# Four of six barriers a layer become waits for data; the beginning, the GDN preparation and the join to the SSM scan put in another order

## The chip, the cores and the metric

The kernel runs on one core of a Trainium2 chip. A core has five engines with an instruction queue each: TensorE (PE, matrix products), VectorE (DVE), ScalarE (ACT), GpSimd (POOL) and SyncE (SP, which here only starts DMA transfers and waits). They meet by semaphores. SBUF has 128 partitions; PE writes into PSUM, here eight banks of 512 f32 a partition. The metric is the time of the whole program on the device in microseconds, lower is better.

## The reference, cut to what matters

One inference step of two layers with three token mixers side by side. There are 1024 latent tokens and 128 context tokens, the model width is 1024.

```python
for l in range(DEPTH):                                   # DEPTH = 2
    shift, scale, gate = modulation(cond, w_mod[l], b_mod[l])   # silu(cond) @ w_mod + b_mod, cond: c and c_ctx
    h = rms_norm(x, norm_w[l]) * (1.0 + scale) + shift
    proj = einsum('btd,de->bte', h, w_in)                # one wide projection, split into all mixers' inputs
    # A: conv, silu, l2_normalize, gated delta rule, forward and backward, in chunks of 64
    o_a = rms_norm(o_f + rev(o_b), gdn_norm_w) * silu(a_z)
    # B: attention of 8 heads over 1152 keys (8 x 128 latent, 128 cached), 2 KV heads, rotary on q and k
    o_att = blocked_attention(q, keys, vals) * silu(b_z)
    # C: Mamba-2 scan, forward and backward, 16 heads of 64, state of 128
    y = rms_norm((y_f + rev(y_b) + ssm_d * c_x) * silu(c_z), ssm_norm_w)
    merged = sigmoid(g_a)*(o_a @ w_branch_a) + sigmoid(g_b)*(o_att @ w_branch_b) + sigmoid(g_c)*(y @ w_branch_c)
    x = x + gate * (merged @ w_out)
y = rms_norm(x, final_norm_w)                            # also returned: k, v and the states of the context
```

The latent tokens' scans begin from given states (`state_gdn`, `state_ssm`).

## The kernel before, in words

**Tiles and program.** The tokens are 9 tiles of 128 (NT = 9): 8 latent ones (NS = 8) and the context tile, number 8. Every engine has its own written program; both layers run in a loop (`Fori(0, DEPTH)`) of the same code. The order on an engine is the order of the code, and between engines only semaphores hold. Wide products are made of three f32r products (`h_hi`, `h_lo` by `w_hi`, `w_lo`, lines 819 to 821 and 1297 to 1299).

**Stages of a layer** (times of layer 1 from the timeline): beginning to 75 us; projection to 1025; GDN preparation 1031 to 1099; attention 1100 to 1360; SSM preparation 1362 to 1476; SSM scan 1477 to 1544; GDN scan 1545 to 1665; branches, gates and output product to about 2007. Between the first six stages stand barriers (line 590, quoted below): an engine drains, counts up `phase_done` and waits until all five have. There are six a layer (NPH = 6): 1 before the GDN preparation, 2 before attention, 3 before the SSM preparation, 4 before the SSM scan, 5 behind it, 6 behind the GDN scan.

```python
def barrier(e, l, k):                                    # line 590
    e.sem_inc(waits_held, 1)
    e.drain().then_inc(phase_done, 1)
    e.wait_ge(phase_done, l * 5 * NPH + 5 * k)
    e.sem_inc(waits_held, 1)
```

**Beginning.** SP loads nine token tiles, then four parts of layer 1's `w_mod` (2 MB each, line 851). PE turns the tokens (1129), makes a modulation product for each part (`mod_product`, 1142: eight k summed one after the other into partitions 0 and 1 of a bank), the norm's sums (1136) between the second and the third, turns 16 blocks of `mod_rows` (1161), and turns the vector constants `vec_in` (1187). ACT copies the products to `mod_rows` (1784). POOL loads the constants (`vec_load`, 22 transfers); `rows` and `qk_gain` are spread over 128 partitions by their DMAs. In layer 2 the modulation has been made during layer 1 with `mod_parts` (1149) and `mod_gather` (1155): 256 columns at a time from `w_next`, the k in four groups of partitions (`k % 4 * 32`), and the groups summed by a product with `pick`.

**GDN preparation.** For each tile PE makes the decay exponents (1318, 1319) from `g_row` and `g_col`, turns the 12 blocks of `gin` (1328) and makes k·k and k·q (1333, 1334); ACT exponentiates (1928) and squares (1936); POOL raises sums to a power; DVE makes the last product into `g_out` (2612); SP stores `g_out` (936), behind six loads into `beta_p` that wait for POOL's `g_clear`.

**Attention** ends with the context tile; **SSM preparation** makes for each tile the masks, `w_ssm`, `x_dt` and `x_rest` (DVE 2767, POOL 2300), the products `y_products` (1442), and beside it the next layer's modulation (`next_columns`). SP stores what the scans need (`tokens_out`). `xy_p_d` is where DVE's and ACT's solved blocks of the GDN are stored.

**SSM scan.** PE turns the first states `s_io` (1505) and makes a step for each tile in both directions: `c_t` by the state (1513), `xs` for its update (1518); POOL makes `s_kept` (2318), DVE the new state (2785). SP loads `xs` and `c_t` (`ssm_loads`, 1015 and 1017). ACT's queue loads the GDN scan's first tiles (`g_XY` by line 707, behind POOL's memsets and `g_clear`, since only blocks on its diagonal are filled), and ACT copies the last context state to `s_io` (2007).

## Time and profile before

| | |
|---|---|
| three runs | 3976.14, 3976.3, 3981.64 us, median 3976.3 |
| the profiled execution | 3979.19 us, its span 3977.4 us |
| granted PE clock | 0.971 of full speed, mean |
| busy PE, PEld | 3704.6 us (93%), 3471.8 us (87%) |
| busy DVE, ACT, POOL | 2056.2 us (52%), 1091.3 us (27%), 666.6 us (17%) |

PE is busy in 93% of the span, but not evenly: in 40 equal slices of it the page gives 6 tenths for the first, 7 for the two with the GDN preparations, 8 or 9 (90% and more) for the others. The chain that ended last tells for each piece of time which engine, queue or transfer the end waited for.

### The profile page before, as it was taken

To read this page: it belongs to the slowest core of one execution; us is meant where nothing else is said; L and a number is where in the kernel's file an instruction comes from. 1 tells how busy PE (TensorE), PEld (TensorE's weight loads), DVE (VectorE), ACT (ScalarE), POOL (GpSimd) and SP (SyncE) were. 2 spreads that over 40 slices of the span, in tenths; PEclk is the share of its full clock that TensorE was granted. 3 is DMA by queue.
4 is the path that set the end of the run, shared out by engine and by line. 5 is a ranking of instruction groups with operands and counts; after the bars stand their busy time and mean duration, and the time that the engine had idled before them with its cause. 6 is when DMAs were issued, how large, how long until landed. Compare 5 with 4: busy or idle time off the path is not lost.

```text
span 3977.4 us, 71786 instructions
## 1 busy us (share of the span) xinstructions
PE 3704.6 (93%) x29139; PEld 3471.8 (87%) x29139; DVE 2056.2 (52%) x2517; ACT 1091.3 (27%) x1952; POOL 666.6 (17%) x738
## 2 busy tenths in 40 slices
PE   6999999999789898899989999999997998988998
PEld 3999999999778775899989999999996886588998
DVE  3631354133478776575365215523326877746743
ACT  3211111122345461322122111111224456232320
POOL 1110111122310133101011101112233003510100
PEclk8999999999899999999989999999998999999999
...
GB/s 227 99 111 90 75 89 87 91 109 118 223 81 39 118 256 261 234 161 95 90 110 111 93 89 84 90 89 105 108 111 222 55 34 237 268 230 194 132 92 88
DMA packets 370673, 516.40 MB, mean 130 GB/s; under 512 B 83088, under 2 KB 293832, under 8 KB 367408
## 3 DMA queue, kind: packets, MB, share of 16 engines
...
q8 instruction: 222, 3.64, 0.4%
...
## 4 chain that ended last, share of the span: by engine, by line
PE 70%; issue 11%; DVE 7%; DMA 4%; DVEq 2%; ACT 2%; POOL 1%; SPq 1%; ACTq 0%; POOLq 0%
PE PSUM L819 10%; PE PSUM L820 10%; PE PSUM L821 10%; PE PSUM L1297 4%; PE PSUM L1299 4%; PE PSUM L1298 4%; PE PSUM L1382 3%; PE PSUM L1369 3%; PE PSUM L1539 2%; PE PSUM L1348 2%; PE PSUM L1671 1%; PE PSUM L1672 1%; PE PSUM L1673 1%; PE PSUM L1349 1%; DMA c_t<-proj_d 1%
## 5 line engine op out<-in xcount | busy, mean ns | idle before, releaser
L819 PE MATMUL PSUM<-h_hi,w_hi 128*128 128x384 f32 x2400 | 807.3, 336 | 8.2 <-DVEq L2513 8.2
L821 PE MATMUL PSUM<-h_hi,w_lo 128*128 128x384 f32 x2400 | 805.0, 335 | 0.0
L820 PE MATMUL PSUM<-h_lo,w_hi 128*128 128x384 f32 x2400 | 805.0, 335 | 0.0
L819 PEld LDWEIGHTS PSUM<-h_hi,w_hi 128*128 128x128 f32 x2400 | 453.3, 189 | 12.7 <-DVEq L2513 8.9
L820 PEld LDWEIGHTS PSUM<-h_lo,w_hi 128*128 128x128 f32 x2400 | 453.3, 189 | 0.0
L821 PEld LDWEIGHTS PSUM<-h_hi,w_lo 128*128 128x128 f32 x2400 | 453.1, 189 | 0.0
L2196 POOL DMA_DIRECT2D proj_d<-leave x140 | 132.3, 945 | 1438.1 <-DVE leave L2509 568.7
L1297 PE MATMUL PSUM<-h_hi,w_hi 128*128 128x384 f32 x960 | 325.1, 339 | 0.0
L1298 PE MATMUL PSUM<-h_lo,w_hi 128*128 128x384 f32 x960 | 321.2, 335 | 0.0
L1299 PE MATMUL PSUM<-h_hi,w_lo 128*128 128x384 f32 x960 | 321.2, 335 | 0.0
L2619 DVE TENSOR_REDUCE row_max<-PSUM 128x1 f32<-128x1152 f32 x128 | 173.4, 1355 | 101.3 <-PE PSUM L1349 101.1
L803 DVE CAST w_hi<-w_raw 128x2048 fp32r<-128x2048 f32 x56 | 68.6, 1224 | 256.3 <-PE PSUM L821 252.0
L1382 PE MATMUL PSUM<-v_all,prob_t 128*64 128x64 f32 x4608 | 165.5, 227 | 20.6 <-DVE o_bz L2696 15.8
L1382 PEld LDWEIGHTS PSUM<-v_all,prob_t 128*64 128x64 f32 x4608 | 148.0, 140 | 41.7 <-issue 21.1
L1297 PEld LDWEIGHTS PSUM<-h_hi,w_hi 128*128 128x128 f32 x960 | 180.4, 188 | 0.1
L1298 PEld LDWEIGHTS PSUM<-h_lo,w_hi 128*128 128x128 f32 x960 | 180.5, 188 | 0.0
L1299 PEld LDWEIGHTS PSUM<-h_hi,w_lo 128*128 128x128 f32 x960 | 180.2, 188 | 0.0
L2512 DVE SCALAR_TENSOR_TENSOR leave<-leave,PSUM 128x1152 f32<-128x1152 f32 x32 | 43.3, 1353 | 260.3 <-ACT leave L1842 260.0
L1348 PE MATMUL PSUM<-k_hi,q_tile 128*128 128x512 f32 (+1 forms) x384 | 145.8, 380 | 17.8 <-SPq L593 11.4
L1369 PE MATMUL PSUM<-cst,prob 128*128 128x128 f32 x1152 | 154.3, 280 | 8.3 <-DVE prob_t L2713 6.2
L1947 ACT ACTIVATE prob<-PSUM,row_max 128x1152 f32<-128x1152 f32 x128 | 155.8, 1217 | 14.9 <-DVE row_max L2619 14.5
L1950 ACT ACTIVATE prob_t<-PSUM 128x640 f32<-128x640 f32 x128 | 90.1, 704 | 247.0 <-PE PSUM L1369 247.0
...
## 6 DMA issues: line engine op xcount, KB each, us to landing
...
```

Source lines behind the costliest of these rows:

```text
L819: pe.matmul(dst, wh, x_hi[:, k, lo:hi], start=(k == 0), stop=False)
L820: pe.matmul(dst, wh, x_lo[:, k, lo:hi], start=False, stop=False)
L821: last = pe.matmul(dst, wl, x_hi[:, k, lo:hi], start=False, stop=(k == kt - 1))
L1297: pe.matmul(dst, wh, h_hi[:, k, at], start=(k == 0), stop=False)
L1298: pe.matmul(dst, wh, h_lo[:, k, at], start=False, stop=False)
L1299: last = pe.matmul(dst, wl, h_hi[:, k, at], start=False, stop=(k == KT - 1))
L1348: pe.matmul(dst, q_tile[t % 2][:, h], k_hi[:, g, col:col + width], start=True, stop=False)
L1369: last = pe.transpose(dst, prob[s][:, j * P:(j + 1) * P], ident)
L1382: last = pe.matmul(bank(7, AD, h * AD)[half], prob_t[s][:, j, half], v_all[:, kt, g * AD:(g + 1) * AD], start=(j == 0), stop=(j == len(sam ...
L1947: act.activation(prob[s][:], PSUM[:, 1536 * s:1536 * s + T], ACT.Exp, bias=row_max[:, t % 2, h:h + 1], accum_out=row_sum[:, t % 2, h:h + 1 ...
L2196: pool.dma_start(proj_d[0:NS, :, one(j * 2 + (blk + b))].rearrange("t p k n -> p t (k n)"), leave[b][:, 0:SAMPLE].rearrange("p (t n) -> p ...
L2619: dve.tensor_reduce(row_max[:, t % 2, h:h + 1], PSUM[:, 1536 * (h % 2):1536 * (h % 2) + T], AX_X, ALU.max, negate=True).then_inc(at_m, 1)
```

## The change

It does the following. (1) NPH becomes 2: the barriers 1 to 4 go, those behind the SSM scan and behind the GDN scan stay. In their place stand waits for single counts of semaphores. (2) Beginning: `mod_product` is gone, `mod_parts` makes 512 columns at a time into banks 4, 5, 0 and 1, and `mod_gather` with `pick` takes the place of the 16 transposes; three gathers stand before the fourth product. DVE writes zeros into these banks first and makes `pick`. `vec_load` has 14 transfers; `rows` and `qk_gain` come in as two rows of `vec_in`, spread by two matmuls, and DVE copies them. POOL's stores of `x_d` wait for `n_t` in place of `n_mm`. (3) GDN preparation: PE turns tile 0 before its decay exponents; POOL raises tile 0's power and issues its row load before the memsets and `g_clear`, and a second `g_clear` follows at tile 5. (4) Attention begins when `gp_v` and `gp_kk` are complete. (5) The SSM preparation begins on `gated`, `ob_out` and `u_done`. (6) SSM scan: PE turns `s_io` ahead of the last `y_products`, into banks 3 to 6; SP asks for `xs` and `c_t` of step 0 at tile 8 of the preparation, ahead of `tokens_out(8)` (their places in SBUF are in another order); POOL's memsets of `g_XY`, `T` and `T6` stand between the `s_kept` of steps 0 to 3.

Of the diff the lines that only number barriers anew, that only take one away, or that repeat a wait of the same kind on another engine are left out, and indentation is cut.

```diff
-NPH = 6
+NPH = 2
...
 for t in range(NT):
     g_store(t)
-barrier(sp, l, 2)
...
+    sp.sem_inc(waits_held, 1)
+for b in range(2):
+    sp.wait_ge(leave_out[b], (l + 1) * 35 * 32)
+    sp.sem_inc(waits_held, 1)
...
+        sp.sem_inc(waits_held, 1)
+        sp.wait_ge(tile_stored, (l * NT + NS) * 64)
+        sp.sem_inc(waits_held, 1)
+        for d in range(2):
+            ssm_loads(0, d)
     tokens_out(t)
 sp.wait_ge(tile_stored, (l + 1) * NT * 64)
-barrier(sp, l, 4)
...
-for t in range(NT):
+sp.sem_inc(waits_held, 1)
...
+sp.wait_ge(sp_dx, l * NT + NT)
...
+for t in range(1, NT):
...
-def mod_product(dst, w):
-    for k in range(KT):
-        last = pe.matmul(dst, cond[:, k:16:8], w[:, k], start=(k == 0), stop=(k == KT - 1))
-    last.then_inc(mod_used, 1)
-def mod_parts(n, w, at=0):
+def mod_parts(n, w, at=0, width=GW):
     for k in range(KT):
         q = k % 4 * 32
-        last = pe.matmul(bank(n, GW, at)[q:q + 2], cond[:, k:16:8], w[:, k], start=(k < 4), stop=(k >= 4))
+        last = pe.matmul(bank(n, width, at)[q:q + 2], cond[:, k:16:8], w[:, k], start=(k < 4), stop=(k >= 4))
     last.then_inc(mod_used, 1)
...
 for g in range(4):
     pe.wait_ge(mod_in[g], 16 if g < 3 else 48)
-    if g >= 2:
-        pe.wait_ge(mod_row, g - 1)
-    mod_product(bank(4 + g % 2)[0:2], w_mod[g])
-    if g == 1:
+    if g == 2:
+        pe.wait_ge(n_add, 1)
+    mod_parts((4, 5, 0, 1)[g], w_mod[g], 0, 2 * GW)
+    if g == 2:
         norm_sums(0)
+        for c in range(3):
+            pe.wait_ge(mod_row, c + 1)
+            mod_gather(mod_rows[:, 512 * c:512 * c + 512], 4, 7, 8 * c)
 pe.wait_ge(mod_row, 4)
-mod_columns(mod_rows, 16, 7, 0).then_inc(mod_used, 1)
+mod_gather(mod_rows[:, 1536:2048], 4, 7, 24).then_inc(mod_used, 1)
...
-pe.transpose(bank(6, NV), vec_in[0:NV], ident[0:NV, 0:NV]).then_inc(vec_t, 1)
+pe.transpose(bank(6, NV), vec_in[0:NV], ident[0:NV, 0:NV])
+for r in range(2):
+    last = pe.matmul(bank(6, P, (r + 1) * P), ident[0:NV + 2, NV + r:NV + r + 1].broadcast_to([NV + 2, P]), vec_in[0:NV + 2], start=True, stop=True)
+last.then_inc(vec_t, 1)
...
-barrier(pe, l, 1)
-for t in range(NT):
+def decay_exponents(t):
     n, p = l * NT + t, t % 2
     pe.wait_ge(gr_in[p], (l * (5 - p) + t // 2 + 1) * 32)
-    pe.wait_ge(gp_e, n)
+    if t:
+        pe.wait_ge(gp_e, n)
+    else:
+        pe.wait_ge(acc_free[1], l * NG + G_ATT + 1)
+        pe.wait_ge(a_q, heads_turned(l, NT, True))
     for d in range(2):
         dst = bank(5 + d).rearrange("p (h t) -> p h t", t=P)
         pe.matmul(dst, ident_r[:], again(far_r[:, d], GH), start=True, stop=False)
         last = pe.matmul(bank(5 + d), g_col[p][:, d], g_row[p][:, d], start=False, stop=True)
     last.then_inc(gp_d, 1)
+for t in range(NT):
+    n, p = l * NT + t, t % 2
+    if t:
+        decay_exponents(t)
     pe.wait_ge(tile_in[p], loaded(l, p, t // 2, 0))
     if t:
         pe.wait_ge(squared, nth(l, t - 1, 1, 4) + 1)
         pe.wait_ge(scaled, l * (3 * NT) + NT + t)
         pe.wait_ge(gp_v, n)
+    else:
+        pe.wait_ge(acc_free[0], l * NG + G_ATT + 1)
     for k in range(12):
         last = pe.transpose(PSUM[:, k * P:(k + 1) * P], gin[p][:, k], ident)
     last.then_inc(transposed, 1)
+    if t == 0:
+        decay_exponents(t)
     pe.wait_ge(gp_kk, n)
     for h in range(GH):
         pe.matmul(bank(3, P, h * P), gin[p][:, 4 + h], gin[p][:, 4 + h], start=True, stop=True)
         last = pe.matmul(bank(4, P, h * P), gin[p][:, 4 + h], gin[p][:, h], start=True, stop=True)
     last.then_inc(gp_k, 1)
-barrier(pe, l, 2)
...
     pe.wait_ge(q_in[t % 2], q_loaded(l, t))
+if t == 0 and h == 0:
+    pe.wait_ge(gp_v, l * NT + NT)
+    pe.wait_ge(gp_kk, l * NT + NT)
...
+if t == 0:
+    pe.wait_ge(gated, nth(l, NS, 0, 3) + 1)
+    pe.sem_inc(waits_held, 1)
...
-pe.wait_ge(sp_yd, (l * NT + NT - 1) * 2)
-next_columns(NS - 1)
-for half in range(2):
-    y_products(NT - 1, half)
-barrier(pe, l, 4)
+pe.wait_ge(sp_e, (l + 1) * NT * 4)
+pe.sem_inc(waits_held, 1)
 for d in range(2):
     pe.wait_ge(state_in[d], l * 32 + 16)
     for b in range(8):
-        last = pe.transpose(PSUM[:, d * 2048 + b * P:d * 2048 + (b + 1) * P], s_io[d][:, b], ident)
+        last = pe.transpose(PSUM[:, 1536 + d * 1024 + b * P:1536 + d * 1024 + (b + 1) * P], s_io[d][:, b], ident)
     last.then_inc(ssm_prod[d], 1)
+pe.wait_ge(sp_yd, (l * NT + NT - 1) * 2)
+pe.sem_inc(waits_held, 1)
+y_products(NT - 1, 0)
+next_columns(NS - 1)
+y_products(NT - 1, 1)
+pe.wait_ge(sp_yd, (l + 1) * (2 * NT))
+pe.sem_inc(waits_held, 1)
...
-for g in range(4):
-    act.wait_ge(mod_used, g + 1)
-    act.activation(mod_rows[0:2, g * 512:(g + 1) * 512], bank(4 + g % 2)[0:2], ACT.Copy).then_inc(mod_row, 1)
+    for g in {4: (0,), KT - 1: (1, 2, 3)}.get(k, ()):
+        act.wait_ge(mod_used, g + 1)
+        act.activation(mod_rows[:, g * 512:(g + 1) * 512], bank((4, 5, 0, 1)[g]), ACT.Copy).then_inc(mod_row, 1)
...
+if t == 0 and d == 0:
+    act.wait_ge(ob_out[half], (l + 1) * (5 - half) * 16)
...
+if t == 0:
+    act.wait_ge(u_done, l * 4 + 4)
...
+act.activation(s_ssm[d][:], PSUM[:, 1536 + d * 1024:2560 + d * 1024], ACT.Copy).then_inc(state[d], 1)
...
-        src = A[name][l].rearrange("d h -> (d h)")
-        pool.dma_start(rows[:, at:at + src.shape[0]], src.partition_broadcast(P)).then_inc(vec_loaded, 16)
-    pool.dma_start(rows[:, 80:96], A["ssm_d"][l].partition_broadcast(P)).then_inc(vec_loaded, 16)
-    for at, name, heads in ((0, "attn_q_norm", AH), (AH, "attn_k_norm", KVH)):
-        for h in range(heads):
-            pool.dma_start(qk_gain[:, at + h], A[name][l].partition_broadcast(P)).then_inc(vec_loaded, 16)
+        src = A[name][l:l + 1].rearrange("o d h -> o (d h)")
+        pool.dma_start(vec_in[NV:NV + 1, at:at + src.shape[1]], src).then_inc(vec_loaded, 16)
+    pool.dma_start(vec_in[NV:NV + 1, 80:96], A["ssm_d"][l:l + 1]).then_inc(vec_loaded, 16)
+    for at, name in ((0, "attn_q_norm"), (AD, "attn_k_norm")):
+        pool.dma_start(vec_in[NV + 1:NV + 2, at:at + AD], A[name][l:l + 1]).then_inc(vec_loaded, 16)
+pool.memset(vec_in[:], 0.0)
+pool.drain()
 vec_load(0)
...
-pool.wait_ge(n_mm, l + 1)
+pool.wait_ge(n_t, l * KT + 1)
...
-barrier(pool, l, 1)
...
-pool.memset(beta_p[:], 0.0)
-pool.memset(u_raw[:, 2], 0.0)
-pool.drain().then_inc(g_clear, 1)
-pool.sem_inc(g_clear, 1)
 for t in range(NT):
+    pool.wait_ge(sums_made, nth(l, t, 1, 4) + 1)
+    pool.tensor_tensor(norm_k[:, t], ss_k[:, t], plus_half[:], ALU.pow).then_inc(inv_rms, 1)
     if t + 2 < NT:
         row_load(t + 2)
-    pool.wait_ge(sums_made, nth(l, t, 1, 4) + 1)
-    pool.tensor_tensor(norm_k[:, t], ss_k[:, t], plus_half[:], ALU.pow).then_inc(inv_rms, 1)
+    if t == 0:
+        pool.memset(beta_p[:], 0.0)
+        pool.memset(u_raw[:, 2], 0.0)
+        pool.drain().then_inc(g_clear, 1)
...
 if t == 5:
     pool.memset(u_sol[:, 2], 0.0)
+    pool.drain().then_inc(g_clear, 1)
...
-barrier(pool, l, 4)
-for n in range(2):
-    for d in range(2):
-        pool.memset(gd[d]["XY"][n][:], 0.0)
-for d in range(2):
-    pool.memset(gd[d]["T"][:], 0.0)
-    pool.memset(gd[d]["T6"][:], 0.0)
-pool.drain().then_inc(g_clear, 1)
+pool.wait_ge(sp_yd, (l + 1) * NT * 2)
+pool.sem_inc(waits_held, 1)
+pool.wait_ge(tile_stored, (l + 1) * NT * 64)
+pool.sem_inc(waits_held, 1)
 for t in range(NS - 1):
+    if 1 <= t < 3:
+        for d in range(2):
+            pool.memset(gd[d]["XY"][t - 1][:], 0.0)
+    elif t == 3:
+        for d in range(2):
+            pool.memset(gd[d]["T"][:], 0.0)
+            pool.memset(gd[d]["T6"][:], 0.0)
+        pool.drain().then_inc(g_clear, 1)
     for d in range(2):
         pool.wait_ge(state[d], l * 17 + t + 1)
         pool.sem_inc(waits_held, 1)
         pool.tensor_tensor(s_kept[d][:].rearrange("p (h q) -> p h q", q=SP_), s_ssm[d][:].rearrange("p (h q) -> p h q", q=SP_),
                            over(e_tot[:, d, scan_tile(t, d), 4:20], SP_), ALU.mult).then_inc(ssm_side[d], 1)
-barrier(pool, l, 5)
...
+for g in range(2):
+    dve.tensor_scalar(bank(4 + g).rearrange("p (c n) -> p c n", n=P), cst[:, C_ID:C_ID + 4], 0.0, None, ALU.mult)
...
+dve.wait_ge(first_c, NT)
+for g in range(2):
+    dve.tensor_scalar(bank(g).rearrange("p (c n) -> p c n", n=P), cst[:, C_ID:C_ID + 4], 0.0, None, ALU.mult)
+dve.tensor_tensor(pick[:], ident[:, 0:2], ident[:, 32:34], ALU.add)
+for q in (64, 96):
+    dve.drain()
+    dve.tensor_tensor(pick[:], pick[:], ident[:, q:q + 2], ALU.add)
...
+dve.tensor_copy(rows[:], bank(6, 96, P))
+dve.tensor_scalar(qk_gain[:, 0:AH], again(bank(6, AD, 2 * P), AH), AD ** -0.5, None, ALU.mult)
+dve.tensor_copy(qk_gain[:, AH:10], again(bank(6, AD, 2 * P + AD), KVH))
...
+dve.wait_ge(g_clear, l * 3 + 2)
...
+else:
+    dve.wait_ge(g_stored[1 - t], (l + 1) * (4 + t) * 16)
...
-for half in range(2):
-    y_sum(NT - 1, half)
+y_sum(NT - 1, 0)
 dve.wait_ge(mod_used, next_done(l, 8))
 dve.tensor_copy(mod[:, 0:16], bank(2, 32, GW).rearrange("p (k c) -> p k c", c=2))
-barrier(dve, l, 4)
+y_sum(NT - 1, 1)
```

What this makes of the order on the engines. First PE at the beginning, of before, from behind the second product: `tmp` is what the norm's sums are made of, `w_mod_256` and `w_mod_261` are the third and fourth part of `w_mod`.

```order
L1136 MATMUL PSUM<-cst,tmp 128x1 [waits n_add]
L1136 MATMUL PSUM<-cst,tmp 128x1 x8
L1142 MATMUL PSUM<-w_mod_256,cond 2x512 [waits mod_row,mod_in2]
L1142 MATMUL PSUM<-w_mod_256,cond 2x512 x7
L1142 MATMUL PSUM<-w_mod_261,cond 2x512 [waits mod_row,mod_in3]
L1142 MATMUL PSUM<-w_mod_261,cond 2x512 x7
L1161 MATMUL PSUM<-cst,mod_rows 128x2 [waits mod_row]
L1161 MATMUL PSUM<-cst,mod_rows 128x2 x15
```

And of the change, from behind the third product; `mod_rows` is what ACT has copied of the products, now from 128 partitions.

```order
L1156 MATMUL PSUM<-cst,tmp 128x1 [waits n_add]
L1156 MATMUL PSUM<-cst,tmp 128x1 x8
L1169 MATMUL PSUM<-pick,mod_rows 128x2 [waits mod_row]
L1169 MATMUL PSUM<-pick,mod_rows 128x2 x3
L1169 MATMUL PSUM<-pick,mod_rows 128x2 [waits mod_row]
L1169 MATMUL PSUM<-pick,mod_rows 128x2 x3
L1169 MATMUL PSUM<-pick,mod_rows 128x2 [waits mod_row]
L1169 MATMUL PSUM<-pick,mod_rows 128x2 x3
L1163 MATMUL PSUM<-w_mod_261,cond 2x512 [waits mod_in3]
L1163 MATMUL PSUM<-w_mod_261,cond 2x512 x7
L1169 MATMUL PSUM<-pick,mod_rows 128x2 [waits mod_row]
L1169 MATMUL PSUM<-pick,mod_rows 128x2 x3
```

The norm's sums have moved behind the third product; three gathers of four matmuls, each behind its copy, come before the fourth product, which waits for its data alone, and one gather stands behind it where 16 transposes stood.

PE where the projection ends and the GDN preparation begins, of before; line 1299 is the projection's last matmul.

```order
L1299 MATMUL PSUM<-h_hi,w_lo_89 128x384
L594 ISA
L1314 ISA [waits phase_done]
L1315 REGISTER_ALU [waits gr_in0]
L1318 MATMUL PSUM<-far_r,ident_r 128x512 [waits gp_e]
L1319 MATMUL PSUM<-g_row_184,g_col_186 128x512
L1318 MATMUL PSUM<-far_r,ident_r 128x512
L1319 MATMUL PSUM<-g_row_184,g_col_186 128x512
L1322 ISA
L1328 MATMUL PSUM<-cst,gin_182 128x128 [waits tile_in0]
L1328 MATMUL PSUM<-cst,gin_182 128x128 x11
```

And of the change.

```order
L1319 MATMUL PSUM<-h_hi,w_lo_89 128x384
L1348 ISA
L1354 REGISTER_ALU [waits tile_in0]
L1356 MATMUL PSUM<-cst,gin_182 128x128 [waits acc_free0]
L1356 MATMUL PSUM<-cst,gin_182 128x128 x11
L1332 ISA
L1340 MATMUL PSUM<-far_r,ident_r 128x512 [waits a_q,acc_free1,gr_in0]
L1341 MATMUL PSUM<-g_row_184,g_col_186 128x512
L1340 MATMUL PSUM<-far_r,ident_r 128x512
L1341 MATMUL PSUM<-g_row_184,g_col_186 128x512
```

The 12 transposes of `gin` stand ahead of the decay exponents, and each of the two has waits of its own in place of `phase_done`.

PE where the SSM preparation ends, of before, from behind the last `y_products`: `s_io` are the first states, `c_t` the tile's input of the scan.

```order
L594 REGISTER_ALU
L1503 ISA [waits phase_done]
L1505 MATMUL PSUM<-cst,s_io_166 128x128 [waits state_in0]
L1505 MATMUL PSUM<-cst,s_io_166 128x128 x7
L1505 MATMUL PSUM<-cst,s_io_167 128x128 [waits state_in1]
L1505 MATMUL PSUM<-cst,s_io_167 128x128 x7
L1521 UNCONDITIONAL_BRANCH
L1521 ISA
L1511 ISA [waits scan_in00]
L1513 MATMUL PSUM<-s_ssm_160,c_t_156 128x512 [waits state0]
```

And of the change: `next_rows` is the next layer's modulation, and lines 1473 are the first of `y_products`' 256 matmuls.

```order
L1169 MATMUL PSUM<-pick,next_rows_145 128x2 [waits mod_row]
L1169 MATMUL PSUM<-pick,next_rows_145 128x2
L1529 ISA
L1532 ISA [waits sp_e]
L1534 MATMUL PSUM<-cst,s_io_166 128x128 [waits state_in0]
L1534 MATMUL PSUM<-cst,s_io_166 128x128 x7
L1534 MATMUL PSUM<-cst,s_io_167 128x128 [waits state_in1]
L1534 MATMUL PSUM<-cst,s_io_167 128x128 x7
L1473 MATMUL PSUM<-x_dt_137,w_ssm_128 64x64 [waits sp_yd,sp_w]
L1473 MATMUL PSUM<-x_dt_137,w_ssm_128 64x64
```

The transposes have moved ahead of the last `y_products` and wait for `sp_e` in place of `phase_done`.

## Rows read from the trace of the kernel before

**Rows 1.** the page, engines' shares of the chain that ended last
```profile
PE 70%; issue 11%; DVE 7%; DMA 4%; DVEq 2%; ACT 2%; POOL 1%; SPq 1%; ACTq 0%; POOLq 0%
```
**Rows 2.** groups by line, whole span: busy us, mean ns, idle before and releaser
```profile
L1513 PE MATMUL PSUM<-s_ssm,c_t 128*128 128x512 f32 x128 | 63.9, 623 | 10.3 <-DMA c_t<-proj_d 10.2
```
**Rows 3.** the chain in order of time, the beginning: start us, us, what
```profile
18.52 20.72 DMA w_mod<-in_w_mod
...
57.92 15.54 PE PSUM L1142 x32
```
**Rows 4.** timeline: start us, us, engine, line, operation, out<-in, [idle before <-releaser]
```profile
35.64 5.43 SPq L851 DMA_DIRECT2D w_mod<-in_w_mod  x1
...
75.20 0.33 PE L1187 MATMUL PSUM<-cst,vec_in 125*128 125x125 f32 x1
...
1457.42 1.05 PE L1149 MATMUL PSUM<-w_next,cond 128*2 128x256 f32 x16
```
**Rows 5.** DMA issues of 37 to 42 us: count, KB each, us to landing
```profile
w_mod<-in_w_mod SPq DMA_DIRECT2D x1, 2048.0 KB, 20.8
```
**Rows 6.** windows: us, busy of PE, PEld, DVE, ACT, POOL, PEclk, DMA share, GB/s
```profile
40.00:45.00 5.00, 5.00 (x8) 0.83 (x7) 4.63 (x5) 3.80 (x4) 0.00 (x0) 0.54 1.04 385
...
1041.00:1099.00 58.00, 39.19 (x249) 35.11 (x247) 41.84 (x73) 24.36 (x55) 18.85 (x23) 0.88 0.87 330
```
**Rows 7.** timeline, projection to GDN preparation
```profile
1024.96 1.13 ACT L1893 ACTIVATE leave<-PSUM 128x1152 f32<-128x1152 f32 x1 [3.59 <-PE PSUM L1299]
...
1031.45 0.79 PE L1318 MATMUL PSUM<-far_r,ident_r 128*128 128x512 f32 x1 [6.52 <-POOLq L593]
...
1035.36 1.02 ACT L1936 ACTIVATE g_sq<-PSUM 128x1024 f32<-128x1024 f32 x1 [0.72 <-PE PSUM L1328]
...
1070.65 0.28 POOL L2243 MEMSET w_inv<- 128x96 f32 x1 [3.75 <-issue]
```
**Rows 8.** line L936's stores, 1020 to 1110: ns min/median/max, first and last start
```profile
L936 SPq DMA_DIRECT2D gdn_tile_d<-g_out x9: 319/320/347, 1041.7 to 1098.8; - x9
...
DMA to landing us min/median/max: 5.0/6.4/9.5
```
**Rows 9.** timeline, to attention and to the SSM preparation
```profile
1098.10 0.69 DVE L2612 TENSOR_TENSOR g_out<-PSUM,g_E 128x512 f32<-128x512 f32 x1
...
1099.59 0.79 PE L1348 MATMUL PSUM<-k_hi,q_tile 128*128 128x512 f32 x1 [5.33 <-SPq L593]
...
1374.23 2.32 POOL L2300 TENSOR_TENSOR x_rest<-xt,dt_rest 128x1024 f32<-128x1024 f32 x1 [2.68 <-DMA xy_p_d<-xy_out]
...
1374.70 2.93 DVE L2767 TENSOR_TENSOR x_rest<-xt,dt_rest 128x1024 f32<-128x1024 f32 x1
```
**Rows 10.** timeline, to the SSM scan, PE
```profile
1471.44 3.95 PE L1442 MATMUL PSUM<-x_dt,w_ssm 128*64 128x64 f32 x128
...
1476.99 1.96 PE L1505 MATMUL PSUM<-cst,s_io 128*128 128x128 f32 x16 [1.60 <-SPq L593]
...
1481.30 3.55 PE L1513 MATMUL PSUM<-s_ssm,c_t 128*128 128x512 f32 x4 [2.34 <-DMA c_t<-proj_d]
...
1489.96 1.88 PE L1513 MATMUL PSUM<-s_ssm,c_t 128*128 128x512 f32 x4
```
**Rows 11.** timeline, SSM scan, POOL, DVE and ACT
```profile
1476.86 3.64 POOL L2307 MEMSET g_XY<- 128x1024 f32 x4 [11.80 <-SPq L593]
...
1482.71 3.76 POOL L2318 TENSOR_TENSOR s_kept<-s_ssm,e_tot 128x1024 f32<-128x1024 f32 x2 [0.34 <-issue]
...
1488.22 2.90 POOL L2318 TENSOR_TENSOR s_kept<-s_ssm,e_tot 128x1024 f32<-128x1024 f32 x1 [1.75 <-DVE s_ssm L2785]
...
1493.99 1.21 DVE L2785 TENSOR_TENSOR s_ssm<-s_kept,PSUM 128x1024 f32<-128x1024 f32 x1
...
1540.84 1.02 ACT L2007 ACTIVATE s_io<-PSUM 128x1024 f32<-128x1024 f32 x1 [60.79 <-PE PSUM L1531]
```
**Rows 12.** line L707's loads on ACT's queue, 1476 to 1540
```profile
L707 ACTq DMA_DIRECT2D g_XY<-xy_d x16: 334/1545/8820, 1487.0 to 1525.3; - x16
```

More of the change, by code:

```diff
@@ L1645, in _ @@
                         y_six(t + 1)
-                barrier(pe, l, 6)
+                barrier(pe, l, 2)
                 def beside(job):
@@ L2724, in _ @@
                 out_gate(NS)
-                barrier(dve, l, 3)
-                for q in range(2):
-                    dve.wait_ge(ob_out[q], (l + 1) * (5 - q) * 16)
-                    dve.sem_inc(waits_held, 1)
                 def y_sum(t, half):
```

76 lines of the change are left out of this document (38 added, 38 removed).

## The prediction

> **What bounds the kernel now.** I read the shares of the chain first: 70% of the chain that ended last is TensorE (PE), 11% issue, 4% DMA, so time is gained only where PE stands still or does work that need not be [rows 1]. Then the groups by line, for what ended PE's idle time: at the first matmul after a join of stages it is often a sequencer's barrier (6.5 us at L1318 [rows 7]), and at L1513, in two layers together, 10.2 us are c_t loads [rows 2]. Then the timeline around each join and the beginning. The program runs two layers; I work out layer 1 and double it. All sums are against the profiled execution (3979.2 us, span 3977.4); the median of the runs is 2.9 us below it, which I take off at the end.
>
> **The beginning.** The chain: the first w_mod lands (39.2 us), four products of 16 matmuls, one after the other, until 73.5, the last two in 15.54, then 16 small transposes and the vec transpose at 75.20 [rows 3, 4]. So a product takes 7.8 us, some of it at half clock. The change sends the eight k of a product to four groups of PSUM partitions (mod_parts). The trace has this form: w_next, 16 matmuls of 256 columns, in 1.05 us [rows 4]; twice the columns give 2.1 us, 4.2 at half clock. Now the landings end last: the fourth w_mod is issued at 35.6 and lands 20.8 later, at 56.4 [rows 4, 5]. PE's new order is products 0, 1, 2, the norm's nine sums, 12 gathers, product 3, 4 gathers. At best product 3 runs from 57.0 to 59.1, then the copy on ScalarE (ACT) 0.6, 4 gathers and the copy to mod 0.8, vec at 60.5: 14.7 us gained. At worst all is at half clock: product 2 (landed at 51, one load of 5.4 us earlier) until 55.3, the sums 4 us, gathers and product 3 until 66.2, vec at 68.2: 7 us. The granted clock was 0.54 of full speed, close to half, in the first 5 us after PE's pause for w_mod [rows 6], and the new PE row has such pauses between products, though shorter ones, so I take a middle 64.0, a gain of 11.2. VectorE (DVE) gets three more small copies ahead of w_hi (rows, two of qk_gain); I estimate them, less what falls away, at twice the 0.33 us in which PE makes 125 such columns, rounded down: minus 0.5. Beginning: **10.7 us (6.5 to 14.2)**. GpSimd's (POOL's) 22 loads become 14 and x_d goes out later, both beside other work. In layer 2 the edit gives nothing (0, or 0.5 lost).
>
> The Trainium skill (TensorE: Matmul & The Clock Gate, Part 3) gives a measured 2.38 times for three column tiles; the two rows above make it 3.7 for four. By 2.38 product 3 would take 3.3 us and the sum would be 1.2 less; the row decides.
>
> **Join 1, projection to GDN preparation.** PE stands 6.5 us until 1031.45, while ACT empties the last accumulator (1024.96 to 1026.1), POOL issues its stores and drains [rows 7]. Now the 12 transposes of gin come first and wait only for the other accumulator and for gin, requested long before: 1024.95 to 1026.5. The four decay matmuls need ACT's copy: until 1027.7. ACT's exps and square (1.0 for the square, as much again and a little for the exps) then end at 1029.9, against 1036.4: 6.5 us. Not all is kept. SyncE's (SP's) stores of g_out stand behind six beta_p loads, and these behind g_clear, that is behind POOL's pow, row_load, two memsets and a drain; a pause that a drain made after such a load was 3.75 us [rows 7]. So g_clear comes at about 1038.5 and the first store at 1041.3, where it is now (1041.7) [rows 8], though its data are ready at 1035. It lands 5.0 us later at best [rows 8]; tile 2 wants its buffer at 1045.1: 1.2 us lost. And nine such stores [rows 8] with the gin and q_tile loads must pass in a stage whose DMA share is 0.87 in 58 us [rows 6]: 50 us of transfers in what would be 52; another 0.3. **5.0 us a layer (0 to 6.6)**; 0 is the case that DMA ends the stage.
>
> **Join 2, to attention.** PE waited 5.3 us, but DVE's last product, which must end in any case, ended at 1098.8; PE began at 1099.59 [rows 9]. **0.7 us a layer (0.4 to 0.8)**. Behind PE's new wait stands only attention, which needs the banks.
>
> **Join 3, to SSM preparation.** PE waited for the barrier here too and may now begin at once, some 2 us earlier. But what ends last in tile 0 is x_rest: POOL waited 2.7 us for the xy_p_d stores, and DVE began its x_rest at 1374.70, 0.5 us after they had landed [rows 9]. SP issues these stores behind its last ob_store, 0.45 us earlier than after the barrier. DVE comes 2 us earlier and then waits for them: from 1374.7 to 1373.8, **0.9 us a layer (0.4 to 2.3)**. ACT's new waits (ob_out, u_done) lie under this.
>
> **Join 4, to the SSM scan.** PE's order was columns of tile 6 (to 1470.5, 1.0 before the y products), of tile 7, y products (1471.44 to 1475.4, two halves of 2.0), barrier, 16 transposes of s_io, copy, wait for c_t; step 0 began at 1481.30 at half clock (3.55 us for four matmuls, 1.88 later), step 1 at 1489.96 [rows 10]. Now: transposes to 1472.5, y half 0 to 1474.5, columns 0.6, half 1 to 1477.1, DVE's y_sum to 1478.0, step 0 at 1478.1. Its xs and c_t are asked for during tile 8, when tile 7's stores have landed and SP has nothing else to issue. With 3.6 us for a direction, step 1 comes at 1485.3: 4.6 us. What is late next: POOL's s_kept (from 1478.0) fits. POOL's memsets, 3.6 us for g_XY and 2.2 for g_T, now stand between the s_kept of steps 0 to 3; s_kept of step 1 ended at 1491.1 and DVE used it at 1494.0, so 1.8 us fit in 2.9 [rows 11]. Of PE's 5.1 us a layer of waits for c_t [rows 2], 2.3 were step 0's; of the other 2.8 I take 1.0, since 1.6 MB are loaded early. **5.6 us a layer (2 to 7.4)**.
>
> The trace shows s_kept at 1.88 us with DVE idle and at 2.90 beside it [rows 11]. The Trainium skill says why (GPSIMD Engine Reference, Specifications): POOL's SBUF interfaces are shared with DVE. By that rule, which speaks against this place, the memsets would stretch to 2.8 us a step, just inside the 2.9; the sum would be the same.
>
> **Sum.** 10.7 + 2 x (5.0 + 0.7 + 0.9 + 5.6) = 35.1 us. 3979.2 - 35.1 = 3944.1, less 2.9: **3941 us**. The two barriers that stay pass a shift on, since all engines come to them and nothing behind them has a time of its own.
>
> **Rivals.**
> (a) DMA takes it back. For: the share of 0.87. Join 1 gives 1.0, join 2 0.7, join 3 0.4, join 4 2: 10.7 + 2 x 4.1 = 19, so 3957. Against: PE's waits in the preparation are for POOL and ACT, not for stores.
> (b) All at its best: 14.2 + 2 x (6.5 + 0.7 + 2 + 7.4) = 47, so 3929. Against: join 3's stores, join 1's beta_p.
> (c) It doesn't do what it says: each new wait ends where the barrier did, on the same late event. Only the beginning's worst is left: 6.5, so 3970. For: nearly so at joins 2 and 3. Against: at joins 1 and 4 the events are 3 to 6 us before the barrier's end.
> (d) Slower. ACT's g_XY loads wait for g_clear, which POOL now gives after step 2's s_kept and the memsets of g_T, at about 1503 instead of 1487. Behind them in ACT's queue stand tile 1's loads, eight more g_XY and the copy of s_io that ends the scan, due at 1535 (1540.84 less 5.6) [rows 11]. The row of loads took 38.7 us before, from 1487.0 to behind 1525.3 [rows 12]; as long again, it ends at 1542, 6 to 7 us a layer late: total 22, 3954. It decides the sign from 50 us on, 17.6 past the room there is. With each of the 16 g_XY at 4 us (1.5 in the middle, 8.8 the longest [rows 12]) it is 69: 36 late a layer, 3941 + 72 = 4013. Against: a g_XY issue takes 0.33 us where the queue is free [rows 12], and DMA has more room before 1503 without them.
>
> **Numbers.** Forecast 3941 (own range 3932 to 3952): 0.70. (a), with the mild form of (d): 0.15. (b): 0.08. (c): 0.04. (d): 0.03. The range 3928 to 3958 holds the forecast, (b) and most of (a). A measurement here can't tell less than 0.2% (8 us) from none; only (c) is near that. Faster 0.93, same 0.04, slower 0.03.
>
> **What would show it.** The vec transpose at 60 to 68 us, with products of 2 to 4 us, the last right behind w_mod 3's landing. First transposes of gin within 0.2 us of the last projection matmul, the first g_out store 10 us or more behind them. PE's first attention matmul 0.1 us after DVE's last g_out. Step 0 of the scan without a wait for c_t, with 1.9 us for four matmuls. The forecast is wrong if GDN preparation, from its first square to attention, grows by over 3 us, if ACT's s_io copy starts later than PE's product it reads, or if x_rest of tile 0 moves by 2 us with PE.

## The result: 29.8 us faster, 0.75%, inside the range and for other reasons than forecast

| | before | the change |
|---|---|---|
| runs, median (lowest to highest) | 3978.97 us (3976.14 to 3984.14) | 3949.14 us (3944.70 to 3957.38) |
| ratio of the runs, 95% interval | | 0.9924 (0.9908 to 0.9941) |
| profiled execution, its span | 3979.19, 3977.4 us | 3957.38, 3955.7 us |

The forecast was 3941 (3928 to 3958). Measured twice more, beside other runs of before, the change came to 3951.09 (before 3986.18; ratio 0.9913, 0.9896 to 0.9929) and 3952.70 (before 3979.25; 0.9938, 0.9924 to 0.9952). The first profile of the change is the slowest of its four executions: the span moved by 21.7 us where the median moved by 29.8. So stages are read below from all profiles that have them, not from one pair.

The chain's shares in the page of the change, which answer to [rows 1]:

```profile
PE 74%; issue 7%; DVE 6%; DMA 5%; SPq 3%; DVEq 2%; POOL 1%; ACT 1%; ACTq 0%; POOLq 0%
```

TensorE's share has grown, and issue has lost 4 points.

**The beginning.** Timeline of the change, answering to [rows 3, 4]: start, length, engine, line; the 16 matmuls of a product are one row.

```profile
26.77 3.59 PE L1163 MATMUL PSUM<-w_mod,cond 128*2 128x512 f32 x16 [4.42 <-DMA w_mod<-in_w_mod]
...
38.64 3.60 PE L1163 MATMUL PSUM<-w_mod,cond 128*2 128x512 f32 x16 [2.93 <-DMA w_mod<-in_w_mod]
42.16 4.00 PE L1156 MATMUL PSUM<-cst,tmp 128*128 128x1 f32 x18
...
46.03 5.26 PE L1169 MATMUL PSUM<-pick,mod_rows 128*128 128x2 f32 x24
...
51.22 3.59 PE L1163 MATMUL PSUM<-w_mod,cond 128*2 128x512 f32 x16
...
56.44 0.30 PE L1204 MATMUL PSUM<-cst,vec_in 125*128 125x125 f32 x1
```

The vec transpose has come from 75.20 to 56.44, more than the forecast's best (60.5). The first product starts at 26.8, while before the first w_mod had not landed until 39.2. The queues in the DMA view, 10 to 30 us: packets, MB, share of 16 engines; first of before, then of the change.

```profile
q0 software_dynamic: 452, 0.37, 66.6%
q1 hardware_dynamic: 511, 1.86, 29.0%
...
x_in<-in_x_sample SPq DMA_DIRECT2D x3, 512.0 KB, 19.4
```

```profile
q1 hardware_dynamic: 2671, 6.65, 94.0%
q0 software_dynamic: 148, 0.00, 0.4%
...
x_in<-in_x_sample SPq DMA_DIRECT2D x4, 512.0 KB, 4.4
```

In before POOL's constant loads, 0.37 MB, held two thirds of the DMA engines' time, and the tokens and w_mod stood behind them: a token tile of 512 KB took 19.4 us to land in place of 4.4. The fourth w_mod landed at 44.0 in place of 56.5. The share of DMA does not tell the two apart (0.91 and 1.00 in before from 10 to 20 and from 20 to 30 us, 0.85 and 1.04 in the change); GB/s does (102 in before from 20 to 30 us, 392 in the change).

From the third product on PE did its new work at the lower of its two levels (1.2 GHz), as windows of the change show (columns as in [rows 6], PEclk before the DMA share):

```profile
38.00:44.00 6.00, 5.36 (x25) 2.25 (x25) 0.00 (x0) 0.60 (x1) 0.00 (x0) 0.50 1.04 388
44.00:51.00 7.00, 7.00 (x35) 7.00 (x34) 2.02 (x10) 0.00 (x0) 1.83 (x1) 0.50 0.82 261
```

**Join 1 and 2.** Timeline of the change, answering to [rows 7, 9], and then the instructions of line 2660 and the stores that answer to [rows 8]:

```profile
1005.09 1.47 PE L1356 MATMUL PSUM<-cst,gin 128*128 128x128 f32 x12
...
1008.72 1.03 ACT L1972 ACTIVATE g_sq<-PSUM 128x1024 f32<-128x1024 f32 x1
...
1017.66 1.75 SPq L946 DMA_DIRECT2D beta_p<-betarow_d  x4
...
1030.14 1.29 DVE L2653 TENSOR_TENSOR g_out<-PSUM,e_rest 128x512 f32<-128x512 f32 x2 [4.40 <-DMA gdn_tile_d<-g_out]
...
1075.18 5.37 POOL L2296 TENSOR_SCALAR s_row<-head_of 128x2048 fp32r<-128x2048 f32 x1 [0.51 <-issue]
...
1080.29 0.77 PE L1380 MATMUL PSUM<-k_hi,q_tile 128*128 128x512 f32 x1 [7.67 <-DVE g_out L2662]
```

```profile
L2660 DVE TENSOR_TENSOR g_E<-g_E,g_E x9: 678/681/3666, 1013.6 to 1075.7; 128x512 f32<-128x512 f32 x9
```

```profile
L942 SPq DMA_DIRECT2D gdn_tile_d<-g_out x9: 319/320/342, 1020.5 to 1080.2; - x9
```

PE now goes on at once (1005.09, right behind the last projection matmul, begun at 1004.92), and ACT's square ends 4.5 us behind that matmul's end, where before it was 11.5. Nothing of it is left at 1080.29: 75.4 us from the last projection matmul to attention, before 75.0. The rows name two losses. SP's first store of g_out goes out at 1020.5, and tile 2, which wants that buffer again, waits 4.4 us on DVE. And the last tile's g_E, begun at 1075.7 beside POOL's s_row, takes 3.67 us in place of 0.68.

There is a third, for which the forecast had no term: the change's second g_clear puts a drain behind POOL's memset of tile 5. POOL's rows on both sides of it:

```profile
1052.67 0.98 POOL L2284 MEMSET u_sol<- 128x1024 f32 x1
...
1058.89 1.03 POOL L2268 TENSOR_TENSOR norm_k<-ss_k,plus_half 128x4 f32<-128x4 f32 x1 [5.24 <-issue]
```

In five of the twelve readings "with" of the table below POOL goes on only 4.85 to 5.6 us behind this memset, and the trace names nothing that it waited for ("issue"), so the drain was what ended last. In the other seven it goes on at 3.5 to 4.8 us, when DVE's sums are there. The five stages took 75.7 us in the mean (75.2 to 76.6), the seven 72.4 (70.0 to 73.3), so much of that stage's scatter goes with this drain. In the kernels with all three edits of set 2 it hardly does (two stages with it, 69.0 and 67.0; four without, 67.4 in the mean), and no run takes the drain away: what it costs is read from traces and not shown.

**Join 3 and 4.** Timeline of the change, answering to [rows 9, 10, 11], and the loads of [rows 12]:

```profile
1357.54 1.23 DVE L2815 TENSOR_TENSOR x_rest<-xt,dt_rest 128x1024 f32<-128x1024 f32 x1 [2.32 <-DMA xy_p_d<-xy_out]
...
1453.29 1.94 PE L1534 MATMUL PSUM<-cst,s_io 128*128 128x128 f32 x16
...
1461.16 1.98 PE L1551 MATMUL PSUM<-s_ssm,c_t 128*128 128x512 f32 x4 [1.36 <-DVE y_acc L2782]
...
1464.70 1.88 PE L1551 MATMUL PSUM<-s_ssm,c_t 128*128 128x512 f32 x4
...
1484.86 4.74 POOL L2358 TENSOR_TENSOR s_kept<-s_ssm,e_tot 128x1024 f32<-128x1024 f32 x2 [2.97 <-issue]
...
1519.43 1.02 ACT L2050 ACTIVATE s_io<-PSUM 128x1024 f32<-128x1024 f32 x1 [61.90 <-PE PSUM L1569]
```

```profile
L711 ACTq DMA_DIRECT2D g_XY<-xy_d x16: 330/474/5757, 1484.8 to 1502.1; - x16
```

Step 0 waits for DVE's last y_sum, no longer for c_t, and runs at full clock (1.98 us, before 3.55).

**The stages over all profiles.** Each is the time between two landmarks on PE, read from the timelines of both layers: from the start of one matmul to the start of the other; mean, with lowest and highest. "Without" are before and two kernels below that keep the barriers (6 readings), "with" are six kernels that have the joins of the change unedited up to the scan (12 readings; 10 in the last row, since one of the six edits the scan).

| stage | without | with | gain a layer | forecast |
|---|---|---|---|---|
| last projection matmul to attention's first | 74.6 (73.7 to 75.5) | 73.8 (70.0 to 76.6) | 0.8 | 5.7 |
| attention, to its last product | 255.6 (253.9 to 257.5) | 255.8 (252.6 to 259.1) | none | 0 |
| to the SSM preparation's first transpose | 8.42 (8.4 to 8.5) | 6.05 (5.9 to 6.4) | 2.4 | with the next two |
| to step 0 of the scan | 118.8 (118.2 to 119.4) | 118.1 (117.3 to 119.1) | 0.7 | |
| to the last c_t product | 57.6 (57.1 to 58.8) | 56.2 (55.1 to 57.5) | 1.4 | 6.5 for the three |

That is 5.3 us a layer, 10.6 in all, where 24.4 was forecast. The first projection matmul of layer 1 stood at 85.2 before (87.3 in `joins_only`, which has the old beginning too) and stands at 65.0 in the mean of the ten profiles with the whole new beginning (61.5 to 67.5): 20.2, where 10.7 was forecast. Together 30.8, against 29.8 measured.

### The profile page after: what moved, and what is told of

Same layout as the page of the kernel before. It is cut to its first block, busy times and chain, and to the rows that moved or that the text cites. A ratio compares the mean times of both kernels' runs of the same rounds, so it can differ in the third digit from the quotient of the medians.

```text
span 3955.7 us, 71725 instructions
## 1 busy us (share of the span) xinstructions
PE 3690.6 (93%) x29163; PEld 3473.9 (88%) x29163; DVE 2066.4 (52%) x2528; ACT 1091.6 (28%) x1952; POOL 647.8 (16%) x712
## 4 chain that ended last, share of the span: by engine, by line
PE 74%; issue 7%; DVE 6%; DMA 5%; SPq 3%; DVEq 2%; POOL 1%; ACT 1%; ACTq 0%; POOLq 0%
PE PSUM L823 10%; PE PSUM L825 10%; PE PSUM L824 10%; PE PSUM L1317 4%; PE PSUM L1318 4%; PE PSUM L1319 4%; PE PSUM L1414 3%; PE PSUM L1577 3%; PE PSUM L1709 2%; PE PSUM L1710 2%; PE PSUM L1711 2%; PE PSUM L1401 2%; PE PSUM L1775 2%; PE PSUM L1776 2%; PE PSUM L1774 2%
```

## The experiments

Kernels of one set ran on one chip beside the same runs of before; times are medians, ratios are to before.

### Set 1: which half gives what (before 3986.18 us)

`after_ref` is the change itself. `begin_only` is before with the beginning of the change, `joins_only` the change with the beginning of before. `loads_only` is before with this part of the beginning alone:

```diff
-src = A[name][l].rearrange("d h -> (d h)")
-pool.dma_start(rows[:, at:at + src.shape[0]], src.partition_broadcast(P)).then_inc(vec_loaded, 16)
+pool.dma_start(vec_in[NV:NV + 1, at:at + src.shape[1]], src).then_inc(vec_loaded, 16)
...
+    last = pe.matmul(bank(6, P, (r + 1) * P), ident[0:NV + 2, NV + r:NV + r + 1].broadcast_to([NV + 2, P]), vec_in[0:NV + 2], start=True, stop=True)
```

> The changed kernel again, as the reference of this set and as a second profile. The first profile of it has a span 21.7 us shorter than that of before, its four runs a median 29.8 us below. Theory A (the profile is one draw of a scatter of some 6 us in runs of one kernel): the stages agree with the first profile within 1 us, but for those in which PE ran at its lower clock; the median is 3944 to 3952. Rival B (the joins gain more than the first profile shows): stages of the layers are shorter than in the first profile by 4 us or more a layer. GDN preparation (from the last projection matmul to the first of attention) 75 us in both theories' first reading; before it was 74.7.

Measured 3951.09. The vec transpose stood at 50.4, 6 us earlier than in the first profile; the stage before attention took 72.6 and 75.3. Theory A on the median; the stages scatter more than its 1 us.

> The kernel before with the change's beginning alone (mod_parts with pick, zeroed banks, 14 constant loads in place of 22, x_d on n_t); all six barriers stay. Theory A (nearly all of the gain is the beginning, the joins give 3 us together): the vec transpose at 56.4 us, the first projection group ends 17.4 us earlier than before, and the median is 17 to 20 us below before (3959 to 3962). Rival B, the forecast's split: the beginning gives 10.7, so the median is 3968 and the joins give the rest.

Measured 3963.86, 22.3 below before (ratio 0.9941, 0.9924 to 0.9957), transpose at 53.5. A, and 2 us more.

> The kernel before with the 14 constant loads alone (rows and qk_gain as two rows of vec_in, spread by two matmuls); the modulation products stay serial, the barriers stay. Theory A (the 15 loads that spread one row over 128 partitions held the DMA engines from 12 to 30 us, at 25 to 170 GB/s with a share near 1, and with them the tokens and w_mod): the first modulation product starts at 26.8 us in place of 39.4, four serial products of 8 us and the sums end near 61, the vec transpose stands at 62 to 63 and the time is 11 to 13 us below before. Rival B (the loads are beside other work, as the forecast had it): the first product stays at 39 and the time within 1 us of before.

Measured 3966.13, 20.0 below before (0.9946, 0.9930 to 0.9963). The timeline of its PE:

```profile
26.00 15.29 PE L1142 MATMUL PSUM<-w_mod,cond 128*2 128x512 f32 x32 [4.43 <-DMA w_mod<-in_w_mod]
...
43.32 13.89 PE L1142 MATMUL PSUM<-w_mod,cond 128*2 128x512 f32 x32
...
58.97 0.33 PE L1187 MATMUL PSUM<-cst,vec_in 125*128 125x125 f32 x1
```

A: the products are the serial ones, and yet the transpose is 16.2 us earlier than in before. A's cause stands and its size was missed: 20.0 us against 11 to 13, the transpose at 59.0 against 62 to 63. The first product starts 13.4 us earlier; the other 2.9 come from the products, 15.29 and 13.89 us for two in place of 16.45 and 15.59, since PE stood at the upper level (2.4 GHz, granted clock 1.00) from 30 to 55 us, where before it was granted 0.54 from 40 to 45 and 0.82 to 0.84 from 55 to 65. Rival B, the forecast's own view, falls.

> The change without its beginning: serial products and 22 loads as before, NPH 2 and all waits and orders at the joins as in the change. Theory A (the joins give 3 to 4 us for both layers together, since the GDN preparation takes back what join 1 and 2 give): median 3972 to 3976, the GDN preparation as long as before or longer. Rival B (the forecast's 24.4 us): median 3953 to 3957.

Measured 3969.98, 16.2 below before (0.9955, 0.9938 to 0.9971); the span was 10.0 below that of before's profile. Neither: more than A's 3 to 4 and less than B's 24. A had read the joins from one profile of the change, that of its longest execution. The table above, with 10.6, stands between, but this run's interval (12 to 25 us) begins just above it; the other difference in this set that shows the joins, `begin_only` less `after_ref`, is 12.8. So the joins are worth 10 to 16 us, by the way they are measured, and B's 24 is refuted by the stages more than by this run alone.

### Set 2: where join 1 and 2 went (before 3978.33 us)

`srow_waits`, `stores_first` and `drain_late` each make one edit to the change, `three_mends` all three. The change itself is not in this set; in the other two it was 35.1 and 26.6 us below before, these four are 30.0 to 36.6 below it. So the stages carry the verdicts here, and set 3 settles the time.

```diff
+pool.wait_ge(gp_kk, (l + 1) * NT)                        # srow_waits
+pool.sem_inc(waits_held, 1)
 pool.tensor_tensor(head_of[:], ident[:, 0:SH], ident[:, SH:32], ALU.add)
...
+g_store(0)                                               # stores_first
+g_store(1)
 sp.wait_ge(g_clear, l * 3 + 1)
...
-        pool.drain().then_inc(g_clear, 1)                # drain_late: ahead of s_kept of step 3
...
+    if t == 3:                                           # and here behind it
+        pool.drain().then_inc(g_clear, 1)
```

> The change, with one wait more: POOL fills s_row only when DVE has made the last g_out (gp_kk), as the barrier before attention had it. In the profiles of the change DVE's g_E of the last tile takes 2.1 to 3.7 us in place of 0.68, beside POOL's s_row of 5.37. Theory A (they share a way to SBUF, and it costs the end of the stage): every g_E takes 0.68, the stage from the last projection matmul to the first of attention is 70 to 72.5 us in place of 72.6 to 76.2, 2 to 3 us a layer, and 4 to 6 us of the time. Rival B (the long g_E comes from something else, or s_row takes the same from the beginning of attention): g_E stays long in one tile, or the attention stage grows by what is gained.

Measured 3946.27 (0.9911, 0.9894 to 0.9927). The stage took 73.1 and 67.9 us, 70.5 in the mean against 73.8; the first of them lies within the change's own scatter. Its end is clearer: from POOL's last norm_k to attention it was 6.8 us in all twelve readings "with" and is 3.8 and 4.8 here. Line 2662 is g_E in it:

```profile
L2662 DVE TENSOR_TENSOR g_E<-g_E,g_E x9: 681/681/683, 1011.7 to 1074.5; 128x512 f32<-128x512 f32 x9
```

No g_E is long any more, and attention did not grow (254.6 and 254.8). A: POOL's s_row held DVE. The Trainium skill says the same (SBUF — State Buffer, Who interferes with whom): DVE and GpSimd share a pair of SBUF ports as an exclusive lock, and the order of issue decides who waits; a DVE instruction with two SBUF inputs contends with a GpSimd one that reads SBUF. g_E has two such inputs and s_row reads SBUF and began first, so by that rule g_E waits; the change's trace agrees. But g_E did not wait for the whole of it as the trace draws it: it was done at 1079.4, while s_row is drawn until 1080.55 (POOL's spans are rough).

> The change, with SP storing g_out of tiles 0 and 1 ahead of the six beta_p loads that wait for g_clear. In the profiles of the change DVE and ACT wait in tile 2 for the landing of the first g_out store, DVE 3.7 to 5.8 us and ACT 5.4 to 7.5. Theory A (the store stands behind beta_p, that behind g_clear): the first store is issued 5 to 6 us earlier, the wait in tile 2 goes, the stage is 3 to 5 us shorter a layer (69 to 72 us). Rival B (DMA ends the stage: a transfer more than is moved in that time must wait for another): the waits move to later tiles and the stage keeps 72.6 to 76 us.

Measured 3946.63 (0.9921, 0.9905 to 0.9938). Its stores of g_out:

```profile
L942 SPq DMA_DIRECT2D gdn_tile_d<-g_out x9: 319/320/341, 1010.3 to 1071.4; - x9
```

The first goes out 10.2 us behind the last projection matmul (1000.1), in the change 15.6, and lands in 5.4 us in place of 9.6. The wait in tile 2 is gone: from the third norm_k of POOL to the fourth it takes 6.6 us in both layers, in the twelve readings "with" 9.6 to 12.8. The stage took 71.4 and 70.6, 2.8 less than their mean, while the long g_E stayed. A in its cause, just under its 3 to 5 us in size.

> The change, with POOL's drain and g_clear of the SSM scan behind the s_kept of step 3 in place of ahead of them. In the first profile of the change POOL stood 2.97 us in that drain and DVE took the new state of step 3 some 1.5 us late. Theory A (the drain is on the scan's chain): the scan, step 0 to the last c_t product, 54 to 55 us in place of 55.1 to 57.5. Rival B (c_t's landings bound the scan): the scan keeps 55 to 57.5 and PE's waits for c_t grow by what the drain no longer costs. Forecast rival (d), that g_XY's loads come late, would show in a later s_io copy in this run: I expect none.

Measured 3948.31 (0.9922, 0.9905 to 0.9939). The scan took 55.7 and 56.0, as in the change, and PE waited for c_t as there (3.5 and 3.7 us; 3.0 to 4.3 in the other kernels "with"): A falls, and of B what it says of the scan holds. The drain that stood 2.97 us in the trace is not what ends the scan. Its s_io copy was not late.

> The three edits together (s_row behind gp_kk, the first two g_out stores ahead of beta_p, the drain behind s_kept of step 3). Theory A (three separate costs): the stage before attention 67 to 70 us, the scan 54 to 55, the time 10 to 16 us below that of the change (3951 beside a before of 3986). Rival B (DMA): 3 to 6 us below it, all of it by s_row.

Measured 3941.75 (0.9905, 0.9889 to 0.9922); the stage 69.0 and 67.5, the scan 56.4 and 55.0. Against the change's 3949 to 3953 in the other sets that is 7 to 11 below it, at or under the low end of A's 10 to 16; set 3 measures it on one chip.

### Set 3: a version to keep, and the forecast's own case (before 3979.25 us)

`after_again` is the change, `mends_again` is `three_mends`. `sp_moves` adds to the latter two moves on SP's queue:

```diff
+    if t == NS:
+        sp.wait_ge(xy_done, l * 4 + 4)
+        sp.sem_inc(waits_held, 1)
+        xy_stores(0)
     ob_store(t, t % 2)
...
-next_load(0)
-next_load(1)
 for t in range(NT):
...
         xin_load(t + 2, t % 2)
+    if t == 0:
+        next_load(0)
+        next_load(1)
```

> The changed kernel, as the reference for the versions beside it. 26 to 35 us below before (ratio 0.991 to 0.9935), the stage before attention 70 to 76 us, vec transpose at 50 to 56.

Measured 3952.70 (0.9938, 0.9924 to 0.9952), stages 76.6 and 73.0, transpose at 51.1.

> The change with the three edits (s_row behind gp_kk, two g_out stores ahead of beta_p, the drain behind s_kept of step 3), against the change on the same chip. Theory A (two of them each give back a part of join 1 and 2): 5 to 12 us below the change, stage before attention 67 to 70 us. Rival B (nothing that a measurement of this kernel tells): within 4 us of the change, with a stage of 72 and more.

Measured 3942.18 (0.9907, 0.9892 to 0.9922), 10.5 below the change on the same chip: its runs lie from 3938.58 to 3944.31, those of the change from 3949.99 to 3957.62. The stage took 67.8 and 67.0. A. The run takes the three edits together; `drain_late` gives no sign that the third has a part in it.

> The three edits, and two moves on SP's queue: the xy stores of direction 0 go out ahead of the last o_bz store, and xin of tile 2 is asked for ahead of the two w_next loads. Theory A (join 3 is bound by SP's queue: the xy_p_d stores and what stands behind them come 16.4 to 16.8 us earlier than in before where PE comes 18.9 earlier): from attention's last product to step 0 of the scan 120 to 122.5 us in place of 123.7 to 125.1, 2 to 4 us a layer, 4 to 8 of the time. Rival B (DMA and DVE bound the preparation anyway): 123.5 to 125, and PE's waits are only put elsewhere.

Measured 3934.84 (0.9894, 0.9878 to 0.9910), the fastest of all, 44.4 below before. From attention's last product to step 0 it took 122.6 and 122.8 us, in the three-edit kernel 123.1 to 125.3. That is some 1.6 a layer and just outside what A expected, and less than half of the 7.3 us between the medians. The rest lies in stages that the edit does not touch, and goes with PE's clock. The runs' mean granted clocks are 0.973 to 0.977, those of `mends_again` 0.971 to 0.973. In the two profiles (spans 3928.4 and 3940.5), from the end of layer 1's scan to layer 2's last projection matmul PE is busy for 1373.8 us in place of 1379.8 with the same 9092 matmuls. So the fastest time may be in good part a draw of the clock; whether the edit has a part in it no run here shows. That SP's queue holds the beginning of the SSM preparation is made likely, not shown: POOL's x_rest of tile 0 starts 17.9 us behind attention's last product, in the three-edit kernel 20.3 to 21.5, but two moves were made at once.

> The change with the 22 constant loads of before (rows and qk_gain spread by their DMAs); products, gathers and joins as in the change. The forecast had costed the loads at nothing and put the vec transpose at 64.0 (60.5 to 68.2), since the fourth w_mod lands at 56.4. Theory A (the forecast's working of the products was right and only the loads were mis-sized): the first product at 38 to 41, the transpose at 60 to 68. Rival B (the products as parts gain by themselves what was measured): it stays at 50 to 57. Time by A 8 to 14 us above the change.

This is the change with only the constants loaded as in before (and so without the two matmuls and DVE's copies that spread them). Measured 3963.18 (0.9961, 0.9948 to 0.9975), 10.5 above the change. Its PE:

```profile
40.12 3.44 PE L1163 MATMUL PSUM<-w_mod,cond 128*2 128x512 f32 x16 [3.12 <-DMA w_mod<-in_w_mod]
...
58.85 5.26 PE L1169 MATMUL PSUM<-pick,mod_rows 128*128 128x2 f32 x24
64.04 3.42 PE L1163 MATMUL PSUM<-w_mod,cond 128*2 128x512 f32 x16
...
69.10 0.30 PE L1204 MATMUL PSUM<-cst,vec_in 125*128 125x125 f32 x1
```

A: with the old loads the transpose comes at 69.1, 1 us behind the forecast's worst case of 68.2 and the 60 to 68 of A, and 15 behind the mean of the kernels with the new loads (53.9).

## Why the forecast was in its range, and what in it was wrong

**The sign and the sum held, the split did not.** Two errors of opposite sign nearly cancel: the beginning gave 9.5 us more than its term, the joins 13.8 less. That the sum lies in its range is luck, and no proof of the working. Two of the forecast's own signs say so too. The vec transpose came at 50.4 to 56.4 and not at 60 to 68. And the GDN preparation from its first square to attention, which was to grow by no more than 3 us, went from 63.2 to 70.0 in the means of the two groups of the table, 6.8 us: by that sign the forecast was wrong about this stage.

**The beginning: the step that failed is "POOL's 22 loads become 14 ... both beside other work".** They were not beside it: they bounded it. Costed at nothing, they move the transpose by 16.2 us alone (`loads_only`) and by 15 on top of the products; in time that was 20.0 and 10.5 us, each known to some 6. The rows to find it were in the trace of before, in the DMA view of 10 to 30 us. I had taken the landing of the fourth w_mod at 56.4 as given, and it was itself late by these loads. One hint was at hand: a first w_mod of 2 MB that took 20.72 us to land [rows 3], with no other w_mod ahead of it; in the change it takes 10.7.

**The products: right mechanism, the worst case's size.** With the old loads they gained 6.1 (75.2 to 69.1, or 8.2 from the 77.3 of `joins_only`); the forecast took 11.2 between 7 and 14.7. From the third product on PE's work stands at half clock there, as the worst case had it: 3.4 to 3.6 us for a product, 4.0 for the sums. Larger than even the worst case had them were the first three gathers, 24 matmuls in the trace: 5.26 us, where it leaves some 2.7 (66.2 less 59.3, the sums' end, and 4.2 for the product). And the landing did not end last: with the old loads the fourth w_mod was there at 56.8, and its product began at 64.04, behind the gathers. The choice of the middle was the error.

The Trainium skill's measured 2.38 times for three column tiles (TensorE: Matmul & The Clock Gate, Part 3), which the forecast put at 3.3 us a product and did not take, comes close to the 3.4 to 3.6 of the trace. It would have put the sum 1.2 lower, also too high.

DVE's copies cost 1.1 us between the transpose and the first projection matmul (11.1 against 10.0), 0.5 was forecast.

**Join 1: the step that failed is "it lands 5.0 us later at best".** The first store of g_out was forecast at 1041.3, 16.4 us behind the projection's end, and came 15.6 behind it (1020.5 against 1004.9): as forecast. But [rows 8] offered 5.0, 6.4 and 9.5 us for a landing and I took the best. Tile 2's wait ended 9.6 us behind the issue, at 1030.14, so DVE lost 4.4 us (2.7 to 5.9 in the twelve readings) in place of 1.2. This very store landed in 5.3 us in before and in 6.5 to 10.4 us in the twelve readings; why it takes longer in its new place stays open. That DMA would end the stage, rival (a)'s reason and my bound of 0, is wrong: with the edits the same transfers pass in a stage of 67.6 us (66.8 to 69.0, six readings), 7.0 less than before.

**Join 2: the step "DVE's last product must end in any case" held, but not its time.** PE begins 0.15 us behind that product in place of 0.80, as forecast. But what stood behind the barrier on POOL, s_row, now starts before the product ends and holds DVE for 1.4 to 3.0 us. The forecast asked what stands behind PE's new wait, but not what POOL does without its own.

**Joins 3 and 4: 4.5 of 6.5.** Step 0 was forecast 4.1 us earlier (0.9 and 3.2), and came 3.1 earlier; the scan gave 1.4, where 2.4 was expected from step 1 and from early c_t. PE's waits for c_t are 7.4 us in both layers, before 10.2 [rows 2]: step 0's have gone, the others grew by some 0.9 a layer.

```profile
L1551 PE MATMUL PSUM<-s_ssm,c_t 128*128 128x512 f32 x128 | 61.3, 601 | 10.3 <-DMA c_t<-proj_d 7.4 <-DVE y_acc L2782 2.7 <-DVE s_ssm L2832 0.2
```

POOL's memsets fit between the s_kept, as forecast: the two of a step took 1.84 us and were not stretched to the 2.8 that the forecast's second reading gave them.

**Rivals.** (a) had the joins nearly right in sum (8.2, measured 10.6) by a mechanism that the edits refute. (b) and (c) did not come. (d): g_clear came late as it said, the g_XY loads ran from 1484.8 to 1502.1 with a median issue of 0.47 us in place of 1.5, and the s_io copy did not wait for them.

What stays open: why the beginning scatters by 6 us between profiles that share it (transpose at 50.4 to 56.4), what the drain of tile 5 costs, and how much of the joins' 16.2 us in `joins_only` is chance, since the stages give 10.6.
